# Second half of the memory's value projection moved between the memory's scores and transposes, x's features in another buffer, second maxima ahead of gating

## The reference

```python
h = rms_norm(x, mix_norm[l]);   x = x + hybrid_mixer_2(h, ...)      # 6 MLA heads, 6 GQA heads, gated MLP; y @ w_out
h = rms_norm(x, mem_x_norm[l]); x = x + memory_cross_attention(h, mem, ...)
h = rms_norm(x, ffn_norm[l]);   x = x + conv_gated_ffn(h, ...)

def memory_cross_attention(h, mem, mem_kv_norm, mem_w_q, mem_w_kv, mem_w_o):
    q = (h @ mem_w_q).reshape(B, S, 4, 128)
    kv = rms_norm(mem, mem_kv_norm) @ mem_w_kv      # 256 memory tokens, 1024 columns:
    k = kv[..., :512]; v = kv[..., 512:]            # the first 512 are keys, the others values, 4 heads each
    return block_attention(q, k, v, 128 ** -0.5) @ mem_w_o
```

## Time and profile before

| | us |
|---|---|
| median of 3 runs (2309.27 to 2310.75) | 2310.06 |
| the profiled execution's own time | 2308.6 |
| its span, first to last instruction | 2306.4 |
| TensorE busy / idle in the span | 2255.9 / 50.5 |
| GpSimd, ScalarE, VectorE busy | 1694.4, 1088.5, 1067.5 |

### The profile page before, as it was taken

How to read it: one execution, slowest core, us unless ns; L and a number is a source line. 1 busy time by engine, 2 the same in 40 slices (tenths; PEclk the granted TensorE clock), 3 DMA queues, 4 the chain that set the end, 5 groups by cost and what they waited for, 6 DMA issues and landing times.

```text
span 2306.4 us, 41556 instructions
## 1 busy us (share of the span) xinstructions
PE 2255.9 (98%) x16573; PEld 2056.1 (89%) x16573; DVE 1067.5 (46%) x1871; ACT 1088.5 (47%) x1317; POOL 1694.4 (73%) x1340
## 2 busy tenths in 40 slices
PE   8999999999999999999999999999999999999998
PEld 7888999999988888898999998889898888898887
DVE  3334656323333333455553233334535765534766
ACT  5335444465433533464444734336654335565333
POOL 6998655556799899875564678996467997655996
PEclk9999999999999999999999999999999999999999
DMA  7554533334565555553343355565334556333663
GB/s 247 188 197 147 165 110 111 119 102 146 166 200 183 182 185 198 183 164 96 108 128 111 129 165 183 182 214 142 110 126 133 198 182 186 117 111 114 198 196 122
DMA packets 316525, 359.97 MB, mean 156 GB/s; under 512 B 20772, under 2 KB 295264, under 8 KB 316256
## 3 DMA queue, kind: packets, MB, share of 16 engines
q1 hardware_dynamic: 316026, 357.65, 48.2%
q10 hardware_dynamic: 358, 0.33, 0.0%
HBM read 356.91 MB, written 1.05 MB: 155 GB/s over the span
## 4 chain that ended last, share of the span: by engine, by line
PE 90%; DVE 5%; ACT 3%; POOL 1%; issue 1%; DMA 0%; SPq 0%; ACTq 0%; DVEq 0%
PE ps L778 23%; PE ps L589 21%; PE ps L621 17%; PE ps L626 9%; PE ps L655 4%; PE ps L908 1%; PE ps L890 1%; PE ps L1180 1%; PE ps L671 1%; POOL sb_lo L562 1%; PE ps L911 1%; PE ps L642 1%; PE ps L1232 1%; PE ps L817 1%; DVE sb_hT L1925 1%
## 5 line engine op out<-in xcount | busy, mean ns | idle before, releaser
L562 POOL TENSOR_TENSOR sb_lo<-sb_raw,sb_hi 128x512 fp32r<-128x512 f32 (+1 forms) x1336 | 1694.2, 1301 | 594.2 <-ACT sb_hi L1339 592.5
L1339 ACT ACTIVATE sb_hi<-sb_raw 128x2048 fp32r<-128x2048 f32 (+2 forms) x341 | 639.1, 1876 | 740.0 <-PE ps L626 358.6
L621 PE MATMUL ps<-sb_hT,sb_hi 128*128 128x512 f32 x1792 | 426.0, 390 | 0.0
L621 PEld LDWEIGHTS ps<-sb_hT,sb_hi 128*128 128x128 f32 x1792 | 332.7, 188 | 66.6
L778 PE MATMUL ps<-sb_hT,sb_hi 128*128 128x256 f32 x2304 | 309.0, 287 | 4.5 <-DVE sb_hT L2189 2.8
L778 PEld LDWEIGHTS ps<-sb_hT,sb_hi 128*128 128x128 f32 x2304 | 284.9, 191 | 10.6 <-DVE sb_hT L2189 3.2
L626 PEld LDWEIGHTS ps<-sb_hT,sb_lo 128*128 128x128 f32 x1792 | 229.8, 191 | 8.7
L1937 DVE TENSOR_TENSOR sb_yinv<-ps,sb_row 128x512 f32<-128x512 f32 x112 | 77.5, 692 | 337.2 <-PE ps L626 336.4
L626 PE MATMUL ps<-sb_hT,sb_lo 128*128 128x256 f32 x1792 | 232.4, 283 | 0.0
L589 PE MATMUL ps<-sb_hi,sb_o_h 128*128 128x512 f32 x560 | 219.8, 392 | 0.4 <-DVE sb_o_l L1944 0.4
L589 PE MATMUL ps<-sb_hi,sb_o_l 128*128 128x512 f32 x560 | 218.7, 390 | 0.0
(11 more groups left out here) (398 smaller groups left out, 3348.5 us busy)
## 6 DMA issues: line engine op xcount, KB each, us to landing
sb_raw<-in_ffn_w_in SPq DMA_DIRECT2D x88, 1024.0 KB, 5.1
sb_raw<-in_w_in SPq DMA_DIRECT2D x76, 1024.0 KB, 5.2
sb_raw<-in_ffn_w_out SPq DMA_DIRECT2D x44, 1024.0 KB, 5.0
sb_raw<-in_ffn_w_up SPq DMA_DIRECT2D x44, 1024.0 KB, 5.1
sb_raw<-in_ffn_w_down SPq DMA_DIRECT2D x22, 1024.0 KB, 4.9
sb_raw<-in_w_out SPq DMA_DIRECT2D x16, 1024.0 KB, 5.2
sb_raw<-in_w_branch_a SPq DMA_DIRECT2D x8, 1024.0 KB, 5.2
sb_raw<-in_w_branch_b SPq DMA_DIRECT2D x8, 1024.0 KB, 5.3
```

The costliest lines, as they stand in the source:

```text
L562: ins = nc.gpsimd.tensor_tensor(lo[:, slot, c], raw[:, slot, c], hi[:, slot, c].bitcast(F32), ALU.subtract)
L621: mm(ps[:, bank + i, :].rearrange("p (h n) -> p h n", h=2), wh[:, c, i * P:(i + 1) * P], hT_both[:, :, c, :], start=c == 0, stop=False, sk ...
L1339: fn(hi[:, slot, 0:width], raw[:, slot, 0:width], ACT.Copy).then_inc(hi_ready, 1)
```

## The change

1. The last value unit of `mem_w_kv` leaves the mixer's plan. It becomes unit 18 (`MEM_V1`), behind the query units, which are now 16 and 17; `w_out` is 12 to 15. TensorE runs three of its four parts after the memory's s1, in the place of the 20 transposes, and the fourth between t0 and t1. ScalarE copies it out after t0's copy. t1 goes to banks 2 and 3, since the unit uses bank 6.
2. Because this unit still reads the memory's features in `o_h` and `o_l`, x's features go elsewhere: the first two pairs to `sb_early`, which lies in the memory of `vT`, the other two to `hT`.
3. ScalarE splits units 18, 19 and 20 in `enter` and right after it: one more than before.
4. The mixer's plan has 12 parts instead of 16, with weights of its own, and VectorE takes the second batch's maxima ahead of the gating.

```diff
-M2_DVE = Steps(["kr", "kpe", "gn", "cn", "gr", "vn", "qr", "qr1", "qr2", "mx0", "mix"]
+M2_DVE = Steps(["kr", "kpe", "gn", "cn", "gr", "vn", "qr", "qr1", "qr2", "mx0", "mx1", "mix"]
...
-MEMORY_BANKS, MEMORY_ROW = (0, 1, 2, 3), 4
+MEMORY_BANKS, MEMORY_ROW, MEM_PT = (0, 1, 2, 3), 4, (4, 2)
...
-MEM_PLAN = plan(range(9, 13), [3] + [MEM_WEIGHT[step] if step in MEM_WEIGHT else {"s": 1.5, "t": 0.3, "v": 1.5}[step[0]]
-                                     for step in scores_order(M2_BATCHES)])
+MEM_WEIGHT = {"s1": 2, "t0": 1, "v0": 1, "v1": 1, "v2": 1, "v3": 1, "v4": 2, "t5": 2}
+MEM_PLAN = plan(range(9, 12), [1] + [MEM_WEIGHT.get(step, 0) for step in scores_order(M2_BATCHES)])
+MEM_OUT, MEM_Q, MEM_V1 = 12, 16, 18
...
+        with nc.sbuf_tensor("sb_early", [P, 2, KB // 2, S], F32R) as early_halves:
+            early_parts = tuple(early_halves[:, i] for i in range(2))
         vT = sb("vT", [P, KB, S])
...
+                load(b, MEM_V1, cols("mem_w_kv_2", l, 256 * 3, 256), 8, 256)
...
+                second_values = quarters(b, MEM_V1, oT, 6, by_token=True)
                 for step in ME_ORDER:
...
-                        pe.wait_ge(mem_kv, 4 * l + 4)
+                        pe.wait_ge(mem_kv, 4 * l + 2)
...
                         if beta == 0:
-                            warm(6)
+                            for _ in range(PARTS - 1):
+                                next(second_values)
                         wv(f"pn{beta}")
-                        weights_out((sqf, rsf)[beta % 2], 4 + bank).then_inc(me_pe, 1)
+                        weights_out((sqf, rsf)[beta % 2], MEM_PT[beta]).then_inc(me_pe, 1)
+                        if beta == 0:
+                            next(second_values)
                     else:
                         wa(f"pt{beta}")
+                        pe.wait_ge(mem_kv, 4 * l + 3 + beta)
...
-                enter(3 * l + (3 * DEPTH + 1), n, q + 3, gain2(V2_MEMX), MEMORY_BANKS, MEMORY_ROW, 3, lambda i: split(b, 19 + i), o_h)
+                enter(3 * l + (3 * DEPTH + 1), n, q + 3, gain2(V2_MEMX), MEMORY_BANKS, MEMORY_ROW, 3, lambda i: split(b, MEM_V1 + i))
+                split(b, MEM_V1 + 2)
...
+                    if step == "t0":
+                        done(b, MEM_V1)
+                        fn(mem_v[:, :, S:2 * S], two(ps[:, 6, :]), ACT.Copy).then_inc(mem_kv, 1)
...
                 top(0)
+                rotated()
+                top(1)
                 mixed()
```

More of the change, by code:

```diff
@@ L182 @@
                       for b in range(M2_BATCHES)], []) + ["seg1"])
-M2_DVE = Steps(["kr", "kpe", "gn", "cn", "gr", "vn", "qr", "qr1", "qr2", "mx0", "mix"]
-               + sum([([f"mx{b + 1}"] if b + 1 < M2_BATCHES else []) + (["segs"] if b == M2_SEG_AFTER + 1 else []) + [f"o{b}"]
+M2_DVE = Steps(["kr", "kpe", "gn", "cn", "gr", "vn", "qr", "qr1", "qr2", "mx0", "mx1", "mix"]
+               + sum([([f"mx{b + 1}"] if 1 <= b < M2_BATCHES - 1 else []) + (["segs"] if b == M2_SEG_AFTER + 1 else []) + [f"o{b}"]
                       for b in range(M2_BATCHES)], []))
@@ L526, in _ @@
                 load(b, 8, rows("mla_w_ukv_2", l, 0, 128), 1, 768)
-                for m in range(4):
+                for m in range(3):
                     load(b, 9 + m, cols("mem_w_kv_2", l, 256 * m, 256), 8, 256)
                 for m in range(4):
-                    load(b, 13 + m, cols("w_out_2", l, 256 * m, 256), 8, 256)
+                    load(b, MEM_OUT + m, cols("w_out_2", l, 256 * m, 256), 8, 256)
                 for m in range(2):
-                    load(b, 17 + m, cols("mem_w_q_2", l, 256 * m, 256), 8, 256)
+                    load(b, MEM_Q + m, cols("mem_w_q_2", l, 256 * m, 256), 8, 256)
+                load(b, MEM_V1, cols("mem_w_kv_2", l, 256 * 3, 256), 8, 256)
                 for m in range(2):
@@ L649, in feature_part @@
                 wh, wl = weights(k, KB, 256)
+                src = src or (lambda c: hT)
                 for i in range(2):
@@ L653, in feature_part @@
                             pe.wait_ge(h_ready, 4 * q + (c // 2 + 1))
-                        for n, (wt, h) in enumerate(((wh, src[0]), (wl, src[0]), (wh, src[1]))):
+                        h_, l_ = src(c)
+                        for n, (wt, h) in enumerate(((wh, h_), (wl, h_), (wh, l_))):
                             ins = mm(ps[:, bank, i * S:(i + 1) * S], wt[:, c, i * P:(i + 1) * P], h[:, c, :],
@@ L680, in turn_row, with enter @@
                 ins.then_inc(row_turned, 1)
-            def enter(e, n, q, b, units, banks, row_bank, early, landed=True, src=(hT_h, hT_l)):
+            def enter(e, n, q, b, units, banks, row_bank, early, landed=True, src=None):
                 (u0, bank0), (u1, bank1) = units
@@ L1258, in mixer2 @@
                         pe.wait_ge(x_ready, 4 * n + (m - 1))
-                        for _ in quarters(b, 13 + m, hT, 4 + m % 2, by_token=True):
+                        for _ in quarters(b, MEM_OUT + m, hT, 4 + m % 2, by_token=True):
                             pass
@@ L1267, in memory @@
                 n = 3 * l + (3 * DEPTH + 1)
-                enter(3 * l + (3 * DEPTH + 1), n, q + 3, b, ((17, 6), (18, 7)), MEMORY_BANKS, MEMORY_ROW, 3, src=oT)
+                enter(3 * l + (3 * DEPTH + 1), n, q + 3, b, ((MEM_Q, 6), (MEM_Q + 1, 7)), MEMORY_BANKS, MEMORY_ROW, 3,
+                      src=lambda c: early_parts if c < 4 else hT)
+                second_values = quarters(b, MEM_V1, oT, 6, by_token=True)
                 for step in ME_ORDER:
@@ L1825, in memory @@
                 two = lambda v: v.rearrange("p (k n) -> p k n", n=S)
-                two_next(b, 15)
-                high_pair(q + 3, 0, gain2(V2_MEMX), o_h, MEMORY_BANKS[0])
-                two_next(b, 16)
+                two_next(b, MEM_OUT + 2)
+                high_pair(q + 3, 0, gain2(V2_MEMX), early_parts[0], MEMORY_BANKS[0])
+                two_next(b, MEM_OUT + 3)
                 for g in range(1, 3):
-                    high_pair(q + 3, g, gain2(V2_MEMX), o_h, MEMORY_BANKS[g])
-                enter(3 * l + (3 * DEPTH + 1), n, q + 3, gain2(V2_MEMX), MEMORY_BANKS, MEMORY_ROW, 3, lambda i: split(b, 19 + i), o_h)
+                    high_pair(q + 3, g, gain2(V2_MEMX), early_parts[0] if g < 2 else hT_h, MEMORY_BANKS[g])
+                enter(3 * l + (3 * DEPTH + 1), n, q + 3, gain2(V2_MEMX), MEMORY_BANKS, MEMORY_ROW, 3, lambda i: split(b, MEM_V1 + i))
+                split(b, MEM_V1 + 2)
                 def out_high(beta):
@@ L1835, in out_high @@
                     sig(fn(o_h[:, 2 * beta:2 * beta + 2, :], two(ps[:, 2 * beta, :]), ACT.Copy))
-                for _ in attention(ME_ORDER, wp, wv, sig, lambda n: P ** -0.5, (kT[:, 4:8, :], zT[:, 0:4, :]), (4, 6), out_high):
-                    pass
+                softmaxes = attention(ME_ORDER, wp, wv, sig, lambda n: P ** -0.5, (kT[:, 4:8, :], zT[:, 0:4, :]), MEM_PT, out_high)
+                for step, _ in zip(ME_ORDER, softmaxes):
+                    if step == "t0":
+                        done(b, MEM_V1)
+                        fn(mem_v[:, :, S:2 * S], two(ps[:, 6, :]), ACT.Copy).then_inc(mem_kv, 1)
             def conv_ffn(l, b):
@@ L1890, in _ @@
                 mixer2(l, b, q)
-                for r in range(13, 15):
+                for r in range(MEM_OUT, MEM_OUT + 2):
                     two_next(b, r)
@@ L2395, in mixed @@
                         ins = tt(qT[:, 2 * i:2 * i + 2, :], qT[:, 2 * i:2 * i + 2, :], two(turned_g[i]), ALU.add)
+                def mixed():
                     wp("mix")
@@ L2443, in mixer2 @@
                     if m >= 1:
-                        low_pair(q + 3, m - 1, gain2(V2_MEMX), o_h, o_l, MEMORY_BANKS[m - 1])
+                        low_pair(q + 3, m - 1, gain2(V2_MEMX), *(early_parts if m < 3 else (hT_h, hT_l)), MEMORY_BANKS[m - 1])
             def maxima(beta, wp, sig, dk):
```

19 lines of the change are left out of this document (9 added, 10 removed).

## The result

| | before | after |
|---|---|---|
| median, runs side by side on one chip (6 and 6) | 2308.91 us (2306.03 to 2310.75) | 2315.41 us (2315.10 to 2320.49) |
| ratio after / before, 95% interval | | 1.0037 [1.0027, 1.0047] |
| profiled execution | 2308.6 us | 2320.49 us |
| its span | 2306.4 us | 2318.3 us |

By the ratio the change makes the kernel slower by 0.37%, or 8.5 us (6.2 to 10.9); the two medians are 6.5 us apart. The forecast was 2317.0, and slower: +7.0 on a kernel before of 2310.06, whose median beside the changed kernel was 2308.91.

The account below looks back on a forecast made before the run. TensorE, busy 2255.9 of 2306.4 us, was taken as the bound. Per layer, mixer -2.4, memory +4.4 and mixer clock +1.5 gave +3.5, so +7.0 for two: 2317 us, range 2305 to 2321.

Parts of the forecast that it names:

- Work out of the mixer, and its waits: Mixer, per layer: 48 matmuls leave, -5.76 us; idle before unit 10 2.1, t2 1.3, v4 2.3; net -2.4.
- t2's: Mixer, TensorE's wait before t2 for the third batch's maxima and exponentials: 0.2 to 1.4 us idle, 1.3 taken.
- The clock in the mixer: Mixer: waits of 2.1 and 2.3 us may halve TensorE's clock; one of the two counted per layer, +1.5 us.
- rival C: Both mixer waits bring the clock down and the memory's t0 delay is paid in full: +5.5 per layer, 2321; chance 0.07.
- The memory: Memory attention, per layer: normalisation held up beside GpSimd delays output product +3.0 us, half-speed clock adds 1.4; together +4.4.
- Rival A: Memory normalisation not held up: -3.1 us per layer, 2304, or 2307 with one mixer clock fall; chance 0.23.
- The other buffer, the moved load, the ring: Features' other buffer, moved unit's load and ring one unit further on: no cost, output projection and `enter` as before.
- The second maxima ahead of the gating: Mixer, VectorE: second maxima begin at 1639.71 instead of 1641.32; gating ends at about 1643.7 instead of 1641.3.
- The sum: Per layer -2.4 mixer, +4.4 memory, +1.5 mixer clock: +3.5; +7.0 for two layers, 2317 us, slower; chance 0.48.
- B: Normalisation held up, but mixer clock stays at 1.00 and t2 waits only 0.2: +0.5 per layer, 2311; chance 0.22.

Follow-up runs that it names:

- Experiment 2: Changed kernel with one of the two parts behind v4 moved ahead of it: 2309.96 us, ratio 1.0016 to the kernel before.
- experiment 7: Changed kernel, early split kept, with the normalising instruction also writing out a sum nobody reads: 2308.29 us, ratio 1.0002 to the kernel before.
- Experiment 6: Experiment 4's kernel plus 16 unread transposes in TensorE's wait before the mixer's unit 10: 2300.03 us, ratio 0.9964 to the kernel before.
- experiment 1: Changed kernel with ScalarE's split of unit 20 moved behind the memory's second exponentials: 2309.14 us, ratio 1.0003 to the kernel before.
- experiment 5: Kernel before with only unit 21 split early, ahead of the memory's exponentials: 2315.83 us, ratio 1.0036 to the kernel before.
- Experiment 3: Changed kernel with VectorE's gating ahead of the second maxima again: 2319.17 us, ratio 1.0051 to the kernel before.
- experiment 4: Changed kernel with the late split of unit 20 and one part moved ahead of v4: 2302.75 us, ratio 0.9978 to the kernel before.

## Why the prediction was right

**Work out of the mixer, and its waits.** Forecast -5.76 and idle time 5.7 in place of 2.32. The waits came out as 2.14, 0.60 and 2.17, against 2.1, 1.3 and 2.3, each at the step and from the releaser that was named. Only t2's was mis-sized: 1.3 was taken, near the upper of the bounds 0.2 and 1.4 that the same step gave. Those bounds don't come out of its own terms either: 1.2, 0.17 to 1.28 and 1.9, less 3.3 us of work, are 0.0 to 1.1. At the full clock the mixer is 53.66 - 5.76 - 2.32 + 4.91 = 50.5 us, 3.2 less than before where 2.4 was forecast. Experiment 2 took 1.6 us out of one of these waits.

**The clock in the mixer.** One fall of 1.5 per layer was forecast. The profiled execution shows one in the first layer (52.33 us, about 1.8 over the 50.5) and two in the second, one of them twice as long (55.34 us, about 4.8 over). That is 3.3 per layer and not 1.5: this term of the sum was too small, and rival C was right for half of the layers. Over many executions, instead of one, experiment 7 gives an estimate: its ratio of 1.0002 is +0.5 us, its memories are 1.72 shorter than before, so all the rest is some 2.2 us longer (by the interval, 0.1 to 4.3). If that lies in the two mixers, which no run shows by itself, they are 2.2 longer where the forecast was 1.8 shorter, and the clock takes back everything that they save. Experiment 6 shows a saving that the clock leaves alone: 49.71 us with it at 1.00, one part also standing before v4 there.

**The memory.** Forecast +4.4 per layer, found +4.09 and +4.07. Its parts: normalisation over 4 to 6 us, found 5.09; idle 3.7, found 3.17; output product 3.0 late at the full clock, found 2.5 (17.72 in experiment 2 against 15.20); clock 1.4, found 1.6 (19.29 against 17.72). Counted from the first score, the three parts ended at 7.92 us for 7.83 forecast, and the normalisation at 11.03 for 11.43: it began where it was forecast to, and each of its four steps took 1.27 us (5.09 / 4) where 1.4 was reckoned. Experiments 1 and 5 show the cause from both sides, by taking the second unit away and by adding one where there was none, and experiment 7 shows that the form of the instruction decides. Rival A, 2304 to 2307, fell with that. Where the normalisation is not held up, as in experiments 1 and 7, the ratios are +0.03% and +0.02%, and not the -0.14% to -0.27% of that rival: it had the mixer wrong too.

**The other buffer, the moved load, the ring.** Forecast nothing. The stage between mixer and memory takes 38.37 us in both layers for 38.35 and 38.37, which bears it out.

**The second maxima ahead of the gating.** The prediction took it as it is. Experiment 3 shows that it isn't the cause of the loss: without it the kernel is no faster.

**The sum.** +7.0 forecast, +8.5 (6.2 to 10.9) measured. By the estimate above the mixers hold about 2.2 of it and the memories the other 6.3, where -1.8 and +8.8 were forecast. The errors of 4.0 and -2.5 have opposite signs, so the median is hit better than either term, and that is luck. The stated range, 2305 to 2321, took in B and most of A besides, so that the time lies in it says little by itself; the traces and experiments decide between them. That the memories are at 6.3 by the ratios and at 8.16 in the one profiled execution fits with the clock, which there fell behind both of their waits; where it doesn't fall, as in experiment 2, the two are 5.0 longer.

**What stays open.** Whether a wait brings the clock down was not settled. In the profiled executions, two layers of each, the same wait was followed by half speed in some and not in others:

| wait | in the executions of | followed by half speed |
|---|---|---|
| 2.14 to 2.16 ahead of unit 10 | after, experiments 1, 2, 4, 7 | 9 of 10 (3.4 us, once 6.8) |
| 2.17 before v4 | after, experiments 1, 3, 7 | 5 of 8 (6.8 three times, 3.4 twice) |
| 2.37 before t1 | experiment 3 | 1 of 2 (10.2) |
| 3.17 in the memory | after, experiments 2, 3 | 3 of 6 (3.4) |
| 1.11 before v0 | before, experiment 5 | 2 of 4 (3.4) |

The last row touches the prediction: it read from the one execution of before that gaps of 1.11 and 0.94 leave the clock up, and those of experiment 5 show the first of them followed by half speed. In experiment 7 the clock stayed at 1.00 behind the wait of 2.16 in the first layer. The half-speed stretch at 255.4 in after had no wait ahead of it at all: TensorE was busy for all of 250.0 to 255.4, in part with matmuls of 8x8, and the same instructions kept the clock in before. Experiment 6 filled one wait alone, ahead of unit 10, and the clock stayed up in both layers; no run varied the length of a wait alone, so no rule is given.

## What to carry to other kernels

When an instruction moves on one engine, follow what it releases on the others: here a split that cost ScalarE nothing let GpSimd run 5 us further, into four VectorE instructions on which TensorE waited. Before work that fills a wait is taken out, price the wait with the clock behind it: the wait of 2.17 us before v4 was followed by no loss in one layer and by some 3 us in the other, and 16 unread transposes in a wait of 2.15 bought back about 0.14%. Read the clock in more than one execution, since one can show a fall that the next doesn't have. Where one form of an instruction is blocked by a neighbour, a dearer form of the same operation may be the cheaper one.

## What the runs showed of the hardware that was not expected

- A plain `tensor_scalar` of 128x256 takes 348 ns with GpSimd idle and 1346 ns with GpSimd at work on pieces of 1.26 us each (10.08 / 8): of four in a row one went through per piece (5.09 / 4 = 1.27). With a written sum it takes 0.48 us in the same place.
- The half-speed stretch behind a wait was 3.4 us in most cases, 6.8 in the second mixer of after and 10.2 in the first mixer of experiment 3; behind a wait of 3.17 us without any matmul it did not come at all in experiment 2 (granted clock 1.00 before and after).
- A fall of the clock need not cost half of its length: behind the wait of 1.11 in experiment 5 it lasted 3.4 us and the mixer got 0.2 us longer, since the next wait, 0.94 in before, was gone.
- With no fall of the clock in the second block's mixers and memories of the profiled execution, the runs of experiment 6 lay within 1.5 us, against 5.8 in the kernel before; with 5 runs and 15 this is an observation, not a measurement.
